# Two layers and four recurrence heads written out on every engine, in place of engine loops

## The chip, the core and the metric

The kernel runs on one core of one Trainium2 chip. The metric is the device time of one execution in microseconds (us). The core has five engines with a sequencer each: PE (TensorE), DVE (VectorE), ACT (ScalarE), POOL (GpSimd) and SP (SyncE, which only issues transfers here). The engines have no common program order; they meet only by semaphores.

## The reference

A decoder trunk of two layers over 16 meta tokens and 1024 real ones (L = 1040 positions, width 1024, float32). Cut to what matters:

```python
for layer in range(DEPTH):                                   # DEPTH = 2
    u = _rmsnorm(h, norm_mix[layer])
    proj = u @ w_in[layer]                                   # columns split among three mixers
    hq, hf, hi, hg, dq, dk, dv, fq, fk, fv, ff = jnp.split(proj, split_at, axis=-1)
    o_a = _hgrn2(hq, hf, hi, hg, ...)                        # gated linear recurrence, 4 heads of 128
    o_b = _diff_attn(dq, dk, dv, ...)                        # two softmax maps, 4 heads of 64
    o_c = _fox_attn(fq, fk, fv, ff, ...)                     # forgetting attention, 4 heads of 64
    h = h + jnp.concatenate([o_a, o_b, o_c], axis=-1) @ w_out[layer]
    u = _rmsnorm(h, norm_ffn[layer])
    h = h + _hier_moe(u, ...)                                # top group of 4, then top 2 of its 8 experts
h = _rmsnorm(h, norm_final)
```

The recurrence is S_t = diag(f_t) S_{t-1} + (1 - f_t) i_t^T, o_t = S_t^T q_t, computed chunk by chunk. The experts are SwiGLU blocks of 1024 to 512 to 1024.

## The kernel before

Each engine has one function that holds its whole program, in an order written out by hand; no scheduler moves anything. Sequence positions are cut into T = 9 tiles (16 rows, then eight of 128). A layer is seven phases, and at the end of each every engine but SP's side cases passes `meet`: it adds to the semaphore `met` when its queue is drained and waits until all have done so.

The phases in the order of the program are: the recurrence, head after head (`project` at L1116 for two projections, L1318 for the other two, then nine blocks: PE computes `levels`, a transpose, the outputs and the state's increment at L1335 to L1365; DVE masks and sums them in `within` at L2015 to L2022 and updates the state at L2039; ACT copies out of PSUM at L943 and L947); the value projection; attention of eight heads (PE: `scores` L1212, `turn_weights` L1237, `outputs` L1250, and pieces of the next heads' projections in between at L1141 to L1175; DVE: row maxima L1827, `join` L1837 to L1843, `turned` L1853; ACT: exponentials L809, `turned` L820, `copy_out` L834); the output projection L1439; routing; the experts, two to a round, 17 rounds in each layer, whose number is only known on the chip; and the sum of both experts' rows with the next norm.

Before the change the layers are one hardware loop on each engine (`with pe.Fori(0, depth) as layer`), the recurrence's heads a loop inside it (`with pe.Fori(0, HEADS) as head`), the rounds of experts a third one with a count from memory. The eight attention heads and all tiles are Python loops, so their code is written out. Semaphores only ever count up, so a wait's value depends on the layer and the head, as in

```python
t = layer * HEADS + head
pe.wait_ge(h_at, ONE + t * T + j + 1)
```

```python
def wait_alone(engine, semaphore, value):
    engine.wait_ge(semaphore, value)
    engine.sem_inc(passed, 1)
```

which is an EVENT_SEMAPHORE of its own (L575) behind the FUSED_REGOPS (L574). `Steps.settle` (L222) is DVE's and ACT's wait for their own earlier instruction.

Of the kernel before, what the change touches and what calls it, by code (L numbers as in the profile page):

```python
# [41 lines left out]
HEADS = 4  # L42
# [185 lines left out]
def build(nc, A, out, stop=PHASES, depth=DEPTH):  # L228

    nc.disable_value_cache = True  # L230
    with ExitStack() as ctx:
# [5 lines left out]
        def signal(name):  # L237

            return ctx.enter_context(nc.semaphore(name))
# [268 lines left out]
        met, passed = signal("met"), signal("passed")  # L508
# [62 lines left out]
        def wait_alone(engine, semaphore, value):  # L571

            engine.wait_ge(semaphore, value)  # L574
            engine.sem_inc(passed, 1)  # L575

        def all_met(layer, phase):

            return layer * ((PHASES - 1) * ENG - 1) + (phase + 1) * ENG - 1

        def meet(engine, layer, phase):

            engine.sem_inc(passed, 1)
            engine.drain().then_inc(met, 1)  # L585
            wait_alone(engine, met, all_met(layer, phase))
# [4 lines left out]
        def _(sp):  # L591
# [19 lines left out]
            ):  # L611
                sp.dma_start(dst, src).then_inc(s_par, 16)

            with sp.Fori(0, depth) as layer:

                if stop > 1:

# [7 lines left out]
                if stop > 1:  # L625
                    def load_qk(n):
                        b = n % 2 if n < HEADS + 2 else 1
                        at = BAND_DA + n * 2 * AW
                        w = A["w_in"][layer].rearrange("(k p) c -> p k c", k=KD)
                        sp.dma_start(w_qk[b], w[:, :, at:at + 2 * AW]).then_inc(t_w[b], 16)  # L630

                    load_qk(0)
                    load_qk(1)
                    with sp.Fori(1, HEADS) as head:
                        t = layer * HEADS + head
                        w = A["w_in"][layer].rearrange("(k p) c -> p k c", k=KD)

                        wait_alone(sp, h_q, ONE + t)
                        sp.dma_start(w_fq, w[:, :, bass.ds(head * 4 * HW, 2 * HW)]).then_inc(h_wfq, 16)
                        wait_alone(sp, h_ig, ONE + t * T)  # L640
                        sp.dma_start(w_ig, w[:, :, bass.ds(head * 4 * HW + 2 * HW, 2 * HW)]).then_inc(h_wig, 16)

                    wait_alone(sp, h_q, ONE + layer * HEADS + HEADS)
                    wait_alone(sp, h_ig, ONE + layer * HEADS * T + HEADS * T)
                    if stop > 2:
                        w = A["w_in"][layer].rearrange("(k p) c -> p k c", k=KD)
                        sp.dma_start(w_v, w[:, :, BAND_V:BAND_FF]).then_inc(v_w, 16)
                    meet(sp, layer, 1)
# [74 lines left out]
        def _(act):  # L723
# [151 lines left out]
                act.wait_ge(own, ONE + turn + 1)  # L875
                act.activation(rstd[:, :], lnss[:, :], ACT.Exp, scale=-0.5).then_inc(done, 1)

            with act.Fori(0, depth) as layer:

                meet(act, layer, 0)  # L880

                if stop > 1:
                    wait_alone(act, s_clean, layer * CLEANS + 2)
                    with act.Fori(0, HEADS) as head:
                        t = layer * HEADS + head

                        def copy_ig(j):
# [208 lines left out]
        def _(pe):  # L1097
# [190 lines left out]

            for j in range(T):
                norm_turn(0, 0, j)  # L1290
            with pe.Fori(0, depth) as layer:
                meet(pe, layer, 0)

                if stop > 1:
                    with pe.Fori(0, HEADS) as head:
                        t = layer * HEADS + head
                        pe.wait_ge(h_wfq, t * 16 + 16)
                        pe.wait_ge(h_at, ONE + t * T)
# [289 lines left out]
        def _(pool):  # L1589
# [10 lines left out]
            for b in range(SLOTS // P):  # L1600
                pool.dma_start(xg[b * P:(b + 1) * P, :].rearrange("p (a n) -> p a n", n=P),
                               zeros.unsqueeze(1).to_broadcast([P, D // P, P])).then_inc(s_zfill, 16)
            with pool.Fori(0, depth) as layer:

                wait_alone(pool, met, all_met(layer, 0))
                for phase in range(1, min(5, stop)):
                    if phase == 2:

                        wait_alone(pool, f_d, ONE + layer * 8 + 8)
                        pool.dma_start(decay_rows[0], dh.bitcast(F32)).then_inc(f_st, 16)  # L1610
                        pool.dma_start(decay_rows[1], dl.bitcast(F32)).then_inc(f_st, 16)
                        wait_alone(pool, f_st, layer * 32 + 32)
                    meet(pool, layer, phase)
                if stop > 5:
                    wait_alone(pool, s_zfill, 16 * (SLOTS // P))
                    meet(pool, layer, 5)
                if stop > 6:
                    before = pool.value_load(pairs[0:1, 1:2], min_val=0, max_val=ROUNDS)
                    count = pool.value_load(pairs[0:1, 0:1], min_val=1, max_val=ROUNDS)

                    def fetch(k, i, nth):

                        n = P if k == 0 else SMALL
                        pool.tensor_copy(pick[0:n, k:k + 1], ids[k][0:n, bass.ds(i, 1)]).then_inc(m_pick, 1)
                        wait_alone(pool, m_pick, ONE + nth)
                        pool.indirect_dma_start(
                            out=xb[0:n, k, :], out_offset=None, in_=u_rows[:, :],
                            in_offset=bass.IndirectOffsetOnAxis(ap=pick[0:n, k:k + 1], axis=0)).then_inc(m_x[k], 16)

                    turns, picks = before * 3 + 2 * layer, before * 2 + 2 * layer  # L1630
                    wait_alone(pool, r_u, (layer + 1) * 16 * T)
                    fetch(0, 0, picks + 1)
                    wait_alone(pool, m_xt, ONE + turns + 2)
                    fetch(0, 1, picks + 2)
                    with pool.Fori(0, count) as i:
                        t = before + i
                        turns, picks = t * 3 + 2 * layer + 2, t * 2 + 2 * layer + 2
                        wait_alone(pool, m_xt, ONE + turns - 2)
                        fetch(1, i, picks + 1)
                        wait_alone(pool, m_xt, ONE + turns + 3)  # L1640
                        fetch(0, i + 2, picks + 2)
                    wait_alone(pool, m_x[0], (before + count) * 16 + layer * 32 + 32)
                    meet(pool, layer, 6)
                if stop > 7:
                    for j in range(T):

                        if j == T - 1:
                            wait_alone(pool, c_h, ONE + T + layer * T + 1)
                        for k in range(2):
                            pool.indirect_dma_start(  # L1650
                                out=ya[0:rows(j), j % (T - 1), k, :], out_offset=None, in_=xg[:, :],
                                in_offset=bass.IndirectOffsetOnAxis(ap=dest[0:rows(j), k, j:j + 1], axis=0))\
                                .then_inc(c_y[j // 2], 16)
# [3 lines left out]
        def _(v):  # L1657
# [265 lines left out]
                finish(ALL - 1)  # L1923
                v.wait_ge(t_out, ONE + layer * ALL + ALL)

            with v.Fori(0, depth) as layer:

                meet(v, layer, 0)

# [1 line left out]
                if stop > 1:  # L1931
# [2 lines left out]
                    v.memset(AT, 0.0).then_inc(s_clean, 1)  # L1934
                    v.wait_ge(s_clean, layer * CLEANS + 2)
                    wait_alone(v, h_const, layer * 32 + 32)
                    with v.Fori(0, HEADS) as head:
                        t = layer * HEADS + head
                        hg.begin(t)
                        lbc = lb[:, bass.ds(layer, 1), bass.ds(head, 1)].rearrange("p a b -> p (a b)")  # L1940
# [542 lines left out]
```

## Time and profile before

| what | value |
|---|---|
| median of 3 runs | 3539.92 us (3539.03 to 3543.38) |
| profiled execution | span 3537.6 us from first to last instruction; its own time is not given apart, the median lies 2.3 us over the span |
| PE busy | 3146.2 us, 89% of the span |
| DVE, ACT, POOL busy | 43%, 23%, 5% |
| granted TensorE clock, mean | 0.924 |
| chain that ended last | PE 71%, DVE 11%, DMA 7%, issue 6% |
| phases of layer 1 (from the chain and the windows) | recurrence 36.7 to 387, attention 401 to 939, output projection to 1076, routing to 1154, experts to 1725, sum and norm to 1787.75 |

### The profile page before, as it was taken

The numbers are of one execution on the slowest core, as the hardware profiler recorded it, in microseconds if no ns is written. First come the engines' busy times: TensorE is split into PE (matmuls) and PEld (weight loads), VectorE is DVE, ScalarE is ACT, GpSimd is POOL, SyncE is SP. The second block draws the span as 40 slices with busy tenths as digits, with TensorE's granted clock in tenths as the row PEclk, the third lists the DMA queues.
The fourth block names the chain that finished last, engine by engine and source line by source line (L and its number), as shares of the span: only waits on it lengthen the run. The fifth ranks groups of instructions, "written<-read, shape, count | busy, mean of one in ns | idle before, by whom it ended". The sixth has DMA issues, their size and how long they took to land.

```text
span 3537.6 us, 50939 instructions
## 1 busy us (share of the span) xinstructions
PE 3146.2 (89%) x16912; PEld 2020.5 (57%) x16912; DVE 1528.3 (43%) x2623; ACT 829.5 (23%) x1917; POOL 168.5 (5%) x239
## 2 busy tenths in 40 slices
PE   7999888898895999999689997888998949999995
PEld 5666456676543555555356664566765435555553
DVE  4666435644325232323446663355543252333324
ACT  4333124432110111111233331344321101111113
POOL 1300000000000000000200000000000000000002
PEclk9999999888896999999889999997978969999997
DMA  5910100001003999999710000000010049999996
GB/s 162 254 51 12 43 13 7 8 7 60 12 30 135 405 406 409 409 410 405 301 37 24 24 24 26 7 7 8 15 52 12 36 182 409 406 408 413 408 411 253
DMA packets 136560, 592.59 MB, mean 168 GB/s; under 512 B 13000, under 2 KB 47816, under 8 KB 119016
## 3 DMA queue, kind: packets, MB, share of 16 engines
q1 hardware_dynamic: 105688, 491.42, 35.4%
q0 software_dynamic: 20400, 72.69, 6.2%
q10 hardware_dynamic: 10336, 26.75, 2.0%
q8 instruction: 76, 1.25, 0.1%
q14 instruction: 60, 0.49, 0.0%
HBM read 524.56 MB, written 66.26 MB: 167 GB/s over the span
## 4 chain that ended last, share of the span: by engine, by line
PE 71%; DVE 11%; DMA 7%; issue 6%; ACT 3%; DVEq 1%; POOL 1%; POOLq 0%; ACTq 0%; SPq 0%
PE ps L1116 7%; PE ps L1439 6%; PE ps L1517 6%; PE ps L1523 6%; PE ps L1157 6%; PE ps L1558 5%; PE ps L1548 5%; DMA arena<-w 4%; PE ps L1250 4%; PE ps L1395 3%; PE ps L1212 3%; PE ps L1237 3%; PE ps L1575 2%; PE ps L1335 2%; DMA arena<-u_rows,arena 2%
## 5 line engine op out<-in xcount | busy, mean ns | idle before, releaser
L1157 PE MATMUL ps<-arena 128*128 128x260 f32 x1024 | 289.9, 416 | 4.6 <-DVE arena L1760 2.8
L1116 PE MATMUL ps<-arena 128*128 128x512 f32 (+1 forms) x768 | 259.4, 496 | 7.3 <-ACTq L585 3.6
L1827 DVE TENSOR_REDUCE negmax<-ps 16x1 f32<-16x16 f32 (+8 forms) x216 | 151.3, 704 | 253.9 <-PE ps L1217 253.2
L809 ACT ACTIVATE arena<-ps,negmax 16x16 f32<-16x16 f32 (+8 forms) x216 | 150.8, 699 | 433.6 <-DVE negmax L1827 432.9
L1517 PE MATMUL ps<-arena 128*128 128x512 f32 x544 | 246.5, 606 | 4.4 <-DMA arena<-w 2.1
L1318 PE MATMUL ps<-arena 128*128 128x256 f32 x1024 | 229.6, 382 | 14.4 <-ACT arena L902 14.4
L1558 PE MATMUL ps<-arena 128*64 128x256 f32 x2176 | 242.3, 381 | 0.0
L1523 PE MATMUL ps<-arena 128*128 128x256 f32 x1088 | 240.4, 379 | 0.0
L1548 PE MATMUL ps<-arena 128*128 128x512 f32 x544 | 239.1, 592 | 0.0
L1523 PEld LDWEIGHTS ps<-arena 128*128 128x128 f32 x1088 | 206.7, 190 | 42.6 <-issue 16.3
L1439 PE MATMUL ps<-arena 128*128 128x512 f32 x512 | 222.4, 592 | 0.0
L1318 PEld LDWEIGHTS ps<-arena 128*128 128x128 f32 x1024 | 191.9, 190 | 49.6 <-ACT arena L902 24.0
L1157 PEld LDWEIGHTS ps<-arena 128*128 128x128 f32 x1024 | 189.6, 201 | 42.0 <-issue 20.5
L1558 PEld LDWEIGHTS ps<-arena 128*64 128x64 f32 x2176 | 153.3, 137 | 99.4 <-issue 25.8
L1250 PE MATMUL ps<-arena 128*64 128x128 f32 (+2 forms) x1440 | 203.2, 321 | 7.1 <-ACT arena L834 3.2
L1116 PEld LDWEIGHTS ps<-arena 128*128 128x128 f32 x768 | 130.5, 196 | 137.4 <-issue 134.1
L1517 PEld LDWEIGHTS ps<-arena 128*128 128x128 f32 x544 | 102.0, 193 | 148.2 <-issue 148.2
L1212 PE MATMUL ps<-rounded 128*128 128x512 f32 (+4 forms) x600 | 178.1, 400 | 3.6 <-ACT arena L809 3.6
L1237 PE MATMUL ps<-ident,arena 128*128 128x128 f32 (+2 forms) x720 | 141.5, 314 | 43.9 <-DVE arena L1853 37.5
L2324 DVE TENSOR_SCALAR arena<-arena 128x512 f32<-128x512 f32 x34 | 14.5, 427 | 374.3 <-ACT arena L1042 374.3
L1548 PEld LDWEIGHTS ps<-arena 128*128 128x128 f32 x544 | 100.7, 190 | 113.8 <-issue 113.8
L1439 PEld LDWEIGHTS ps<-arena 128*128 128x128 f32 x512 | 96.0, 190 | 114.8 <-issue 114.8
(345 smaller groups left out, 4182.7 us busy)
## 6 DMA issues: line engine op xcount, KB each, us to landing
arena<-w SPq DMA_DIRECT2D x204, 2048.0 KB, 20.7
xg<-arena POOLq DMA_DIRECT2D x51, 512.0 KB, 12.2
xg<-arena ACTq DMA_DIRECT2D x34, 512.0 KB
arena<-w_in SPq DMA_DIRECT2D x16, 1024.0 KB, 5.6
xg<-arena ACTq DMA_DIRECT2D x68, 128.0 KB, 9.5
arena<-w_in SPq DMA_DIRECT2D x16, 512.0 KB, 4.0
arena<-w_out SPq DMA_DIRECT2D x2, 4096.0 KB, 13.2
u_rows<-arena SPq DMA_DIRECT2D x16, 512.0 KB, 2.6
```

Source lines behind the costliest of these rows:

```text
L1116: mm = pe.matmul(dst[0:hi - lo, a:b], w[:, k, lo:hi], uT[:, k, a:b], start=(k == 0), stop=(k == KD - 1))
L1157: mm = pe.matmul(out, w_qk[b][:, k, :], uT[:, k, lo:hi], start=(k == 0), stop=(k == KD - 1), skip_group_check=True)
L1212: mm = pe.matmul(flat[0:r, side + x:side + y], q[:, cols(j)], k[:, x:y], start=(i == 0), stop=False, skip_group_check=True)
L1237: mm = pe.transpose(ps[0:rows(i), 5, m * P:m * P + r], weights_in(n, j, 0)[0:r, cols(i)], ident[0:r, 0:r])
L1250: mm = pe.matmul(ps[half:half + AW, 7, at:at + r], V[0:rows(i), i, n * AW:(n + 1) * AW], WT[0:rows(i), g % 3, m * P:m * P + r], start=(i < ...
L1318: mm = pe.matmul(ps[0:r, 6 + j % 2, 0:2 * HW], uT[:, k, cols(j)], w_ig[:, k, :], start=(k == 0), stop=(k == KD - 1), skip_group_check=True)
L1439: mm = pe.matmul(ps[:, 3 * (j % 2) + half, :], mT[:, j % 2, k, :], w_o[:, k, half * 512:half * 512 + 512], start=(k == 0), stop=(k == KD - ...
L1517: mm = pe.matmul(ps[:, 0, :], XT[:, c, :], W1[0][:, c, :], start=(c == 0), stop=(c == KD - 1))
L1523: mm = pe.matmul(ps[:, 1 + q, 0:F // 2], XT[:, c, :], W3[0][:, c, q * F // 2:(q + 1) * F // 2], start=(c == 0), stop=(c == KD - 1))
L1548: mm = pe.matmul(ps[:, 3 + half, :], GT[:, c, :], W2[0][:, c, half * 512:half * 512 + 512], start=(c == 0), stop=(c == KF - 1))
L1558: mm = pe.matmul(ps[q * SMALL:(q + 1) * SMALL, 0 if w is W1 else 1, 0:F // 2], XS[:, c, :], w[1][:, c, q * F // 2:(q + 1) * F // 2], start ...
L1827: v.tensor_reduce(negmax[0:r, at:at + 1], flat[0:r, side:side + wide_], AX.X, ALU.max, negate=True)\
```

## The change

`layer` and `head` become Python numbers on all five engines: the loop over the layers is written out twice, and the recurrence's loop over its heads four times in each. Every wait outside the rounds of experts then has a constant value. The loop over the rounds stays, with its registers. `wait_alone` drops its increment where the value is constant.

```diff
@@ -572,7 +572,8 @@
             engine.wait_ge(semaphore, value)
-            engine.sem_inc(passed, 1)
+            if not isinstance(value, int):
+                engine.sem_inc(passed, 1)
@@ -611,7 +612,7 @@
-            with sp.Fori(0, depth) as layer:
+            for layer in range(depth):
@@ -631,7 +632,7 @@
-                    with sp.Fori(1, HEADS) as head:
+                    for head in range(1, HEADS):
...
@@ -1288,12 +1289,12 @@
-            with pe.Fori(0, depth) as layer:
+            for layer in range(depth):
                 meet(pe, layer, 0)
                 if stop > 1:
-                    with pe.Fori(0, HEADS) as head:
+                    for head in range(HEADS):
                         t = layer * HEADS + head
```

The same two edits stand on ACT and DVE, and the first of them on POOL. No matmul, vector operation or transfer is added, removed or moved against another.

PE, one block of the recurrence before (h_ktTc: ACT has copied the transposed keys; h_at: DVE has made the block's attention matrix; h_igc, h_oc: ACT's copies of the projections and of the output; h_S: DVE has the state):

```order
L1351 ISA
L1352 MATMUL ps<-ident,arena 128x128 [waits h_ktTc]
L1354 ISA
L1355 ISA [waits h_at]
L1356 ISA [waits h_igc]
L1358 ISA [waits h_oc]
L1359 MATMUL ps<-arena 128x128 [waits h_S]
L1361 MATMUL ps<-arena 128x128
L1364 ISA
L1365 MATMUL ps<-arena 128x128 [waits h_ktTc]
```

The same place of the change (all its lines are one higher):

```order
L1353 MATMUL ps<-ident,arena 128x128 [waits h_ktTc]
L1360 MATMUL ps<-arena 128x128 [waits h_oc,h_S,h_igc,h_at]
L1362 MATMUL ps<-arena 128x128
L1366 MATMUL ps<-arena 128x128 [waits h_ktTc]
```

```order
L574 ISA
L1175 MATMUL ps<-rounded,gamma_r 128x260 [waits t_qa]
L1176 MATMUL ps<-rounded,gamma_r 128x260
L1235 ISA
L1237 MATMUL ps<-ident,arena 128x128 [waits t_WT]
L1237 MATMUL ps<-ident,arena 128x128 x3
L574 ISA
L574 ISA [waits t_WT]
L1250 MATMUL ps<-arena 64x128 [waits t_oc]
L1250 MATMUL ps<-arena 64x128 x3
L574 ISA
L1168 ISA [waits t_qa]
```

The same place of the change:

```order
L1176 MATMUL ps<-rounded,gamma_r 128x260 [waits t_qa]
L1177 MATMUL ps<-rounded,gamma_r 128x260
L1238 MATMUL ps<-ident,arena 128x128 [waits t_WT]
L1238 MATMUL ps<-ident,arena 128x128 x3
L1251 MATMUL ps<-arena 64x128 [waits t_oc,t_WT]
L1251 MATMUL ps<-arena 64x128 x3
L1170 MATMUL ps<-arena 128x260 [waits t_raw,t_qa]
```

All register instructions are gone, and with them the EVENT_SEMAPHORE behind each L574, which these rows don't show.

DVE in the attention of the last heads before (t_T: PE has turned the weights; t_pv: PE has read the buffer; t_S: scores are ready):

```order
L1850 ISA
L1851 ISA [waits t_T]
L1853 COPY arena<-ps 128x512 [waits t_pv]
L1850 ISA
L1851 ISA [waits t_T]
L1853 COPY arena<-ps 128x128 [waits t_pv]
L1826 ISA
L1827 TENSOR_REDUCE negmax<-ps 128x1 [waits t_S]
```

The same place of the change:

```order
L1854 COPY arena<-ps 128x512 [waits t_pv,t_T]
L1854 COPY arena<-ps 128x128 [waits t_pv,t_T]
L1828 TENSOR_REDUCE negmax<-ps 128x1 [waits t_S]
```

The two register instructions of each copy are gone, and one EVENT_SEMAPHORE that holds the second wait takes their place. In the built programs PE has 960 register instructions and 427 EVENT_SEMAPHORE before, 48 and 756 after, but before they stand inside loops; its whole program goes from 4078 instructions to 7898, ACT's from 1351 to 1971, DVE's from 1859 to 2654.

## Rows read from the trace of the kernel before

**Rows 1.** The page: busy time and shares; granted clock and DMA in 40 slices.
```profile
PE 3146.2 (89%) x16912; PEld 2020.5 (57%) x16912; DVE 1528.3 (43%) x2623; ACT 829.5 (23%) x1917; POOL 168.5 (5%) x239
PEclk9999999888896999999889999997978969999997
DMA  5910100001003999999710000000010049999996
```

**Rows 2.** Windows of attention (both layers, one weak stretch), experts: us, busy us, PEclk, DMA share.
```profile
401.00:943.00 542.00, 472.00 (x2498) 337.97 (x2497) 250.41 (x540) 172.94 (x481) 1.06 (x2) 0.89 0.05 16
880.00:920.00 40.00, 34.93 (x187) 24.43 (x184) 16.98 (x36) 8.86 (x27) 0.00 (x0) 0.71 0.00 1
1154.00:1725.00 571.00, 564.31 (x2752) 326.46 (x2752) 169.15 (x199) 64.68 (x133) 36.27 (x65) 1.00 1.00 401
2153.00:2700.00 547.00, 478.22 (x2494) 342.61 (x2493) 249.92 (x538) 172.87 (x481) 1.10 (x2) 0.87 0.05 16
```

**Rows 3.** Source lines L574, L575, L1355: duration ns min/median/max, first and last start.
```profile
L574 PEldq FUSED_REGOPS  x1010: 37/37/152, 35.3 to 3483.7; - x169
L575 PEldq EVENT_SEMAPHORE  x1010: 51/51/51, 35.9 to 3488.7; - x169
L1355 PEldq FUSED_REGOPS  x72: 102/103/103, 102.3 to 2127.2; - x72
```

**Rows 4.** Waits in the attention of layer 1: us in total, times, longest.
```profile
PEld ps L1250 <- issue: 32.8, 136, 0.9
```

**Rows 5.** Chain in time, attention: start us, us, what.
```profile
490.81 0.05 ACTq L772
...
924.64 0.03 issue
924.67 0.05 DVEq L1851
924.71 0.04 issue
924.76 0.70 DVE arena L1853
925.46 0.04 issue
925.50 0.66 PE ps L1237 x4
...
941.07 0.05 DVEq L2103
```

**Rows 6.** Chain in time, recurrence, head 1's projections to its level operands.
```profile
155.43 0.10 ACTq L927
155.53 0.05 issue
...
160.10 0.03 issue
160.13 0.13 DVEq L1983
160.26 0.05 issue
```

**Rows 7.** Timeline of one block of the recurrence, [idle before <-releaser].
```profile
192.88 0.63 DVE L2015 TENSOR_TENSOR ps<-ps,arena 128x448 f32<-128x448 f32 x1
193.10 0.30 PEld L1359 LDWEIGHTS ps<-arena 128*128 128x128 f32 x2 [0.19 <-DVE arena L2039]
193.42 0.21 DVE L2018 COPY arena<-ps 64x64 f32<-64x64 f32 x1
193.66 1.26 DVE L2022 TENSOR_REDUCE arena<-ps 64x64 f32<-64x448 f32 x2
194.95 0.35 DVE L2039 SCALAR_TENSOR_TENSOR arena<-arena,glast,ps 128x128 f32<-128x128 f32 x1
195.22 0.63 DVE L2015 TENSOR_TENSOR ps<-ps,arena 128x448 f32<-128x448 f32 x1
```

**Rows 8.** Chain in time around the layer's start, first and second layer.
```profile
35.39 0.53 DVEq L585
35.92 0.80 issue
36.72 1.22 PE ps L1116
...
1784.29 0.07 ACTq L878
1784.36 2.42 issue
1786.78 0.03 ACTq L878
```

**Rows 9.** Source lines L1291 and L1296: branches of the layers' and the heads' loop.
```profile
L1291 PEldq COMPARE_BRANCH  x2: 77/1705/3333, 1782.3 to 3534.5; - x2
L1296 PEldq COMPARE_BRANCH  x8: 76/214/242, 121.7 to 2127.8; - x8
```

More of the change, by code:

```diff
@@ L876, in head_rstd @@
                 act.activation(rstd[:, :], lnss[:, :], ACT.Exp, scale=-0.5).then_inc(done, 1)
-            with act.Fori(0, depth) as layer:
+            for layer in range(depth):
                 meet(act, layer, 0)
@@ L884, in _ @@
                     wait_alone(act, s_clean, layer * CLEANS + 2)
-                    with act.Fori(0, HEADS) as head:
+                    for head in range(HEADS):
                         t = layer * HEADS + head
@@ L1290, in _ @@
                 norm_turn(0, 0, j)
-            with pe.Fori(0, depth) as layer:
+            for layer in range(depth):
                 meet(pe, layer, 0)
                 if stop > 1:
-                    with pe.Fori(0, HEADS) as head:
+                    for head in range(HEADS):
                         t = layer * HEADS + head
@@ L1602, in _ @@
                                zeros.unsqueeze(1).to_broadcast([P, D // P, P])).then_inc(s_zfill, 16)
-            with pool.Fori(0, depth) as layer:
+            for layer in range(depth):
                 wait_alone(pool, met, all_met(layer, 0))
@@ L1924, in attend_dve @@
                 v.wait_ge(t_out, ONE + layer * ALL + ALL)
-            with v.Fori(0, depth) as layer:
+            for layer in range(depth):
                 meet(v, layer, 0)
@@ L1936, in _ @@
                     wait_alone(v, h_const, layer * 32 + 32)
-                    with v.Fori(0, HEADS) as head:
+                    for head in range(HEADS):
                         t = layer * HEADS + head
```

## The prediction

> **What bounds the kernel now.** I read the page first, for which engine could be the bound at all: PE is busy for 89% of the span, DVE for 43%, ACT for 23% [rows 1]. The digits of the clock fall below 9 in the middle of each layer, and those of the DMA stand at 9 only in one quarter of each layer. So the kernel is at least two kernels, and I cut it with windows [rows 2]. In the experts the DMA engines are busy for a share of 1.00 over 571 us and PE for 564: weights set that stretch, PE is as good as full too, and its clock is whole. In the attention the DMA has a share of 0.05, DVE works for 250 of 542 us, ACT for 173, PE for 472 at a clock of 0.89; the second layer's is alike (478 of 547). There PE stands still for 70 and 69 us while it waits to and fro with DVE and ACT. Attention is what register work could be delaying. The third view is the chain in order of time, to see what such a wait is made of; the fourth the single source lines of the sequencer's instructions, since the page doesn't count them.
>
> **What a register wait costs.** One FUSED_REGOPS lasts 37 ns on PE in its short form and 103 in its long one (a layer and a head in the value), an EVENT_SEMAPHORE 51 [rows 3]. That they run costs nothing by itself: a sequencer works ahead of its engine. They cost where one of them has to wait for a semaphore, because then everything behind it is held, and after the release the register work still has to be done before the engine starts. In the chain such a handoff shows as four pieces: PE's transposes end at 924.64, DVE's copy starts 120 ns later, behind 0.03 issue, 0.05 DVEq L1851 and 0.04 issue; back to PE, where the wait is on the matmul itself, it takes 40 ns [rows 5]. So about 0.08 us of 0.12 is the register instruction.
>
> **The change part by part.**
>
> *Attention, PE.* Each `outputs` is preceded by one or two pairs L574 and L575, of which the profile has 1010 [rows 3]. PE's weight loads of L1250 stood idle 136 times in this stretch for "issue", that is for nothing but the sequencer, 32.8 us in all or 0.24 each [rows 4]. One pair is 37 + 51 = 88 ns, with some 30 ns to pass from one to the next (the pieces between in [rows 5]) 0.12. After the change the usual case is one constant wait on the matmul itself and no pair; where t_oc stands beside t_WT one EVENT_SEMAPHORE stays, which is about what a second pair costs now. I take one pair saved at each of the 136: 136 x 0.12 = 16 us. Bounds: nothing, if each gap is the array's own pace between matmuls, and 32.8 if all of it is sequencer.
>
> *Attention, DVE and ACT.* I count 46 pieces like those of [rows 5] on layer 1's chain in the attention, 27 on DVE and 19 on ACT, the first at 490.81 us and the last at 941.07 [rows 5]. An EVENT_SEMAPHORE takes the FUSED_REGOPS's place where two waits meet, so 0.07 us each at best: 3 us. Bounds 0 and 46 x 0.12 = 5.5. Attention thus gives 19 us a layer, 38 in both.
>
> *Recurrence, blocks.* Here PE's order loses the most: six long register instructions in a block, of which L1355, L1356 and L1358 stand in a row, 3 x 103 ns and the passes between. PE indeed idles for 0.19 us before L1359 [rows 7]. But the same rows show DVE without an idle bracket: 0.63, 0.21, 1.26 and 0.35 us, one behind the other, and the next block's L2015 starts 2.34 us after the last. Its register instructions lie under its own running operations. DVE sets the block, and a faster PE waits for it: I cost the 56 inner blocks at 0. If DVE only looks full, the three instructions that become two would save some 0.3 a block, 17 us.
>
> *Recurrence, edges of a head.* On the chain are 0.15 us at L927 and 0.18 at L1983 [rows 6], less the 40 ns that any handoff takes; about twice that again lies at the first block (before DVE is saturated) and at the last. I take 0.75 a head, 6 us for eight; bounds 2 and 10.
>
> *Start of a layer.* PE's first matmul starts 0.80 us after the drain in layer 1, behind a branch and five register instructions. In layer 2 the chain has 2.42 us of issue between ACT's branch and its next MOVE [rows 8], and PE's branch lasts 3.33 us instead of 0.08 [rows 9]. Written out, no engine branches back here. I take 0.7 and 2.6, together 3.3. The page "Runtime: NRT & Kernel Launch" of the Trainium skill, section "Instruction fetch mechanics", says that a taken branch out of a window of two 16 KiB pages forces a fetch before execution goes on. By that rule the heads' loop on PE, 24 KB long, might pay as well; the trace has at most 0.24 us for it [rows 9], and PE has work queued in that time, so the rule's larger sum (six times about 3 us more) is not taken.
>
> *Meets, SP, POOL, output projection, routing.* Their waits are short or under other work: 3 us for 14 meets and the tails of both recurrences (bounds 1 and 6). Nothing in the rounds of experts changes but a term of the layer, and the weights set them: 0.
>
> Sum: 38 + 0 + 6 + 3.3 + 3 = 50 us. The profiled span of 3537.6 us becomes 3487.6; with the 2.3 us that the median lies above it, 3490.
>
> **The rivals.**
>
> *More than that (3450).* Each microsecond that PE no longer idles in attention could also keep its clock up. A mean of 0.89 and 0.87 says that it is at the lower level, 1.2 instead of 2.4 GHz, for 22% and 26% of the two stretches, 119 and 142 us [rows 2]. If a quarter of these goes back to the full level, 65 us of work take half as long, 32 less; with half of the recurrence's bound of 17 for its blocks that is 40, so 3450. For: the weak stretches are those in which PE idles. Against: DVE's full row.
>
> *Mostly hidden (3525).* The gaps before L1250 are then the array's pace, and what PE gains is given to waits for ACT's and DVE's operations, which don't get shorter. Remain the layer's start 3, edges 6, handoffs 3 and meets 3: 15 us. For: PE's FUSED_REGOPS mostly run while matmuls are queued. Against: the 136 gaps have no releaser.
>
> *Instruction fetch takes it back (3540, no change).* The changed program is longer: three more copies of each head's body, twice, are some 15 pages of 256 instructions over PE, DVE and ACT, that before were run from what was loaded. If each cost the 3.33 us of the branch [rows 9] that would be 50 us, all of the gain. Against: attention is straight code already, of which thousands of instructions are run without a gap of that size, and in layer 2 everything is loaded again today.
>
> *Slower (3585).* Attention holds a mean clock of 0.89 and 0.87, but in 880 to 920 us only 0.71, with PE hardly less busy than elsewhere [rows 2]. If a changed rhythm of short bursts and waits took the mean to 0.80, 475 us of PE's work would become 0.88/0.80 of that, 47 us a layer more, 95 in both against 50 gained. It decides from a mean of 0.835 downwards. Nothing in the change makes gaps longer, so it is unlikely.
>
> **How the numbers follow.** Forecast 0.66, more 0.14, mostly hidden 0.13, fetch 0.04, slower 0.03. The forecast's own range is 3465 to 3515, from attention's two bounds taken by halves. To leave out no more than 2 in 10 the whole range reaches toward both neighbours: 3456 to 3522. Less than 0.2% (7 us) can't be told from no change in this kernel. Faster 0.92 (the first three, less 0.01 for a hidden case hidden further), same 0.05, slower 0.03.
>
> **What would show it.** Right: attention some 20 us shorter in each layer at PE busy about the same; the wait of L1250 for issue falling from 32.8 to about 17; L1851's piece gone or replaced by one of 0.02; blocks of the recurrence still 2.34 us apart, with more idle before L1359; layer 2's first L1116 within about 1 us of ACT's last copy; rounds of experts as long as before. Wrong: blocks clearly shorter than 2.34 (DVE was held by its registers after all), an attention that moves by under 8 us or over 35, gaps of 1 us and more on PE with no releaser in heads 1 to 3 (fetch), or a mean clock in attention away from 0.88 by more than 0.03.

## The result and the profile after

The changed kernel takes 3513.07 us in the median of four runs (3501.87 to 3519.85), the kernel before 3541.65 beside it (3539.03 to 3561.24). The ratio of the runs that were timed beside each other is 0.9901 with a 95% interval of 0.9876 to 0.9927: 35 us less (26 to 44); the two medians differ by 28.6. One execution of the kernel before, in the last set of runs below, was disturbed (4214.6 us at a clock of 0.72) and stands in no other figure. The profiled execution took 3514.0 us with a span of 3511.6, 26.0 less than the span of before. I had forecast 3490, 50 us less.

The page of the changed kernel, to be held against [rows 1] (all lines of the code are one higher now): its head, the chain by engine, the clock in 40 slices, and the queue that loads instructions.

```profile
span 3511.6 us, 44842 instructions
...
PE 3132.8 (89%) x16912; PEld 2012.4 (57%) x16912; DVE 1527.0 (43%) x2623; ACT 830.8 (24%) x1917; POOL 169.7 (5%) x239
...
PEclk8999999897796999999889999997987969999997
...
q8 instruction: 94, 1.54, 0.2%
...
PE 67%; DVE 17%; DMA 8%; ACT 4%; issue 4%; POOL 1%; POOLq 0%; SPq 0%; ACTq 0%; DVEq 0%; PEldq 0%
```

The same engine instructions are executed, and every engine's busy time is the same but PE's, which is 13 us less. Issue on the chain has gone from 6% to 4%, and DVEq from 1% to 0%. In layer 1's attention the chain of before has 184 pieces with DVEq or ACTq, 8.7 us of them, and that of the changed kernel 24, 0.5 us. DVE's share rose from 11% to 17%, in part because the chain of the recurrence's blocks, which ran through PE's matmuls before (134.8 of 139 us), runs through DVE's operations now (99.0). The windows say where the time went (window, its length in us, busy us of PE, PEld, DVE, ACT, POOL, the mean granted clock, DMA share): attention of both layers, the weak stretch, the experts.

```profile
399.94:937.53 537.59, 474.26 (x2575) 339.69 (x2572) 251.93 (x543) 173.77 (x481) 1.06 (x2) 0.89 0.05 16
2140.76:2681.66 540.90, 479.01 (x2575) 342.76 (x2572) 252.08 (x543) 173.78 (x481) 1.11 (x2) 0.88 0.05 16
...
1143.00:1720.00 577.00, 565.88 (x2759) 326.64 (x2758) 168.80 (x198) 64.36 (x132) 37.49 (x66) 1.00 0.99 396
879.00:919.00 40.00, 34.89 (x196) 24.63 (x192) 17.49 (x36) 7.97 (x23) 0.00 (x0) 0.72 0.00 1
```

[Rows 2] have windows that end elsewhere. With the same two landmarks, from the first L1157 to the first L1439, the kernel before shows:

```profile
400.76:948.65 547.89, 477.89 (x2575) 340.99 (x2571) 252.11 (x543) 173.21 (x481) 1.06 (x2) 0.88 0.05 16
2152.04:2706.12 554.08, 485.30 (x2574) 346.47 (x2571) 252.17 (x543) 173.23 (x481) 1.10 (x2) 0.87 0.05 16
```

So attention is 10.3 and 13.2 us shorter, 23.5 of the 26. Of these PE's idle time (length less busy, both layers) makes 13.6, from 138.8 to 125.2, and its busy time 9.9. The rest by landmarks: the recurrence, from L1116's first to L1374's first matmul, is 352.9 and 353.4 us before, 353.1 and 352.4 after; the first layer's start is 0.9 us shorter, the second's with the norm before it 2.4 (59.8 to 57.4); the experts, from the first L1517 to the last L1575, 592.0 and 589.9 before, 595.8 and 589.3 after, a change that I don't count, since the kernels below have 588 to 599 there, with nothing altered in the experts.

Two readings of single waits. First the row that my largest term rested on, [rows 4], in the changed kernel (engine, line, what it waited for, us, times, longest):

```profile
PEld ps L1251 <- issue: 28.5, 123, 0.5
```

It had 32.8 us and 136 times. I had it fall to 17. In the trace of before matmuls are running during 29.9 of the 32.8 us, so that PE itself stands still for 2.8 of them; in the changed kernel it does for 0.9. Second, the handoff of [rows 5], PE's transposes to DVE's copy and back, in the chain (start us, us, what):

```profile
904.97 0.23 PE ps L1238
905.20 0.02 issue
905.22 0.70 DVE arena L1854
905.92 0.04 issue
905.97 0.90 PE ps L1238 x3
```

DVEq L1851 and one issue of it are gone: 20 ns where 120 were.

Start of the second layer, as [rows 8], and one block of the recurrence on DVE, as [rows 7] (start us, us, engine, line):

```profile
1776.72 0.02 ACT arena L1091
1776.74 0.06 issue
1776.81 0.56 ACTq L586
1777.36 0.04 issue
1777.40 2.07 PE ps L1117 x2
```

```profile
191.58 0.63 DVE L2016 TENSOR_TENSOR ps<-ps,arena 128x448 f32<-128x448 f32 x1
191.77 0.30 PEld L1360 LDWEIGHTS ps<-arena 128*128 128x128 f32 x2 [0.24 <-issue]
...
192.11 0.21 DVE L2019 COPY arena<-ps 64x64 f32<-64x64 f32 x1
192.35 1.26 DVE L2023 TENSOR_REDUCE arena<-ps 64x64 f32<-64x448 f32 x2
...
193.64 0.35 DVE L2040 SCALAR_TENSOR_TENSOR arena<-arena,glast,ps 128x128 f32<-128x128 f32 x1
...
193.90 0.63 DVE L2016 TENSOR_TENSOR ps<-ps,arena 128x448 f32<-128x448 f32 x1
```

ACT's last copy is followed by a matmul after 0.66 us where 2.42 of issue lay alone; this block takes 2.32 us instead of 2.34 (in the median of all 2.33 instead of 2.34), with PE's weight loads idle for 0.24 before its output instead of 0.19.

### The profile page after: what moved, and what is told of

Read it like the earlier page. It is cut to its first block, busy times and chain, and to the rows that moved or that the text cites. A ratio compares the mean times of both kernels' runs of the same rounds, so it can differ in the third digit from the quotient of the medians.

```text
span 3511.6 us, 44842 instructions
## 1 busy us (share of the span) xinstructions
PE 3132.8 (89%) x16912; PEld 2012.4 (57%) x16912; DVE 1527.0 (43%) x2623; ACT 830.8 (24%) x1917; POOL 169.7 (5%) x239
## 3 DMA queue, kind: packets, MB, share of 16 engines
q8 instruction: 94, 1.54, 0.2%
## 4 chain that ended last, share of the span: by engine, by line
PE 67%; DVE 17%; DMA 8%; ACT 4%; issue 4%; POOL 1%; POOLq 0%; SPq 0%; ACTq 0%; DVEq 0%; PEldq 0%
PE ps L1117 7%; PE ps L1518 7%; PE ps L1524 6%; DMA arena<-w 6%; PE ps L1440 6%; PE ps L1158 6%; PE ps L1559 5%; PE ps L1549 4%; PE ps L1251 4%; PE ps L1396 3%; PE ps L1213 3%; PE ps L1238 3%; PE ps L1576 2%; DVE negmax L1828 2%; PE ps L1319 2%
```

## The experiments

Twelve kernels were timed in interleaved rounds beside the kernel before. Its median was 3545.66 us beside *layers_only*, *pe_only*, *dve_act_only* and *keep_increment* (23 runs), 3547.43 beside the four with more register instructions in the attention (31), and 3542.17 beside *late_last*, *heads_only* and the two of the recurrence (35). Ratios are given with their 95% intervals.

### Which part: layers, heads, engines, increments

*layers_only*: the loop over the layers is written out on all engines, the four heads of the recurrence stay a loop.

```diff
-            with pe.Fori(0, depth) as layer:
+            for layer in range(depth):
...
                     with pe.Fori(0, HEADS) as head:
```

> The layers are written out on every engine, the recurrence's four heads stay a loop; waits of attention, projection and routing are constants, those of the recurrence still come from a register. If the gain sits in the attention and at the layer's start, as the two traces suggest (attention 10 and 13 us shorter, start 3.4), this kernel keeps nearly all of it: span 3512 to 3516, attention 528 and 531 us, layer 1's recurrence as before at 353 us from the first L1116 to the first L1374. Rival (my forecast's 0.75 us at each head's edge, or a code path that is only good in one straight piece): span 3518 to 3525, with the loss in the recurrence. Rival (the loop over heads costs instruction fetch): the recurrence 1 to 3 us longer a head than with everything written out.

It took 3515.97 us, a ratio of 0.9917 (0.9897 to 0.9937); the span of the profiled run is 3509.8. The heads are 85.43, 85.36 and 85.38 us long, no longer than with everything written out. The whole gain is there within the intervals; writing out the heads has no part that can be seen. The clock has none either: the mean granted clock over the runs is 0.9212, against 0.9210 of the kernel before beside it.

*heads_only*: the complement, the recurrence's heads written out, the layers a loop.

```diff
             with pe.Fori(0, depth) as layer:
...
-                    with pe.Fori(0, HEADS) as head:
+                    for head in range(HEADS):
```

> The recurrence's four heads are written out on every engine, the layers stay a loop, so that all values still come from a register of the layer, and every branch of the heads' loop is gone. With the layers alone written out the whole gain was there already (ratio 0.9917), so this should give nothing that can be measured: within 4 us of before, heads of 85.3 to 85.9 us. My forecast's term for the edges of a head (0.75 us each) would be 2 to 6 us, if the branch rather than the register values were its cause. If it is slower by more than 5 us, the longer program costs something by itself.

It took 3552.92 us, 1.0020 (1.0002 to 1.0038). There is no gain, as expected, but a trace of a loss, to which I come with the clock. The recurrence is 354.9 and 355.1 us long.

*pe_only* has both edits on PE alone.

> Only PE is written out, in layers and heads; DVE, ACT, POOL and SP keep their loops and register values. Theory A (PE's register instructions and the pairs L574 and L575 hold PE's sequencer in the attention): most of the gain stands, attention 530 and 534 us, span 3516 to 3522. Theory B (the handoffs count, that is the register instruction behind each release on DVE and ACT): PE gives little, attention 535 and 541, span 3528 to 3534. In both the recurrence stays at 353 us a layer, since DVE sets its blocks.

It took 3532.61 us, 0.9959 (0.9941 to 0.9977), 14 us less (8 to 21). That is neither theory's number, but about half of the gain.

*dve_act_only* has them on DVE and ACT alone.

> Only DVE and ACT are written out, in layers and heads; PE, POOL and SP keep their loops. The mirror of the kernel with PE alone. Theory A (PE's sequencer): little here, attention 536 and 542 us, span 3530 to 3535. Theory B (handoffs on DVE and ACT): most of the gain, attention 531 and 535 us, span 3518 to 3524. If the two halves add up to the whole (26 us of span), the costs lie one behind the other on one chain; if each alone gives nearly all, one hides the other; if each gives little, both must go together.

It took 3533.78 us, 0.9961 (0.9945 to 0.9977), 14 us less (8 to 20), again about half. The two halves add up to about 28 of the 29 to 35 that the kernels with all engines win. So PE's share and that of DVE and ACT lie one behind the other as far as these intervals tell, and are of one size. My forecast for the attention had 32 to 6. The mean clock is 0.9208 and 0.9207 in these two, as good as that of before.

*keep_increment*: everything written out, but the helper keeps its increment for constants too.

```diff
             engine.wait_ge(semaphore, value)
-            if not isinstance(value, int):
-                engine.sem_inc(passed, 1)
+            engine.sem_inc(passed, 1)
```

> Everything is written out as in the changed kernel, but a wait through the helper still adds one to its own semaphore, so on PE some 1010 EVENT_SEMAPHORE of 51 ns stay, now in front of every output, and none of these waits can ride on a matmul. If the instruction behind the pair is what held PE (half of the pair's time), half of the attention's gain is lost: attention 533 and 537 us, span 3520 to 3526. If the register instruction alone held it, attention 529 and 532 us, span within 3 us of 3511.6. If PE's sequencer runs so far ahead that neither counts, the same 3511.6.

It took 3513.87 us, 0.9906 (0.9884 to 0.9928), which can't be told from the changed kernel. Yet the row before the outputs is almost that of before:

```profile
PEld ps L1250 <- issue: 31.7, 129, 0.8
```

So 3 us more of "issue" in that row cost nothing that the times can tell. Matmuls are running during 28.8 of these 31.7 us: nine tenths of the row are idle time of PEld, not of PE. That the EVENT_SEMAPHORE behind the wait is free is not shown. PE idles for 129.3 us in both attentions against 125.2 in the changed kernel, and the mean clock of this kernel's six runs is high, 0.9242 against 0.9210 beside it, so a price of some 5 us may be hidden.

### Number of register instructions, or their place

Four kernels are the one before with more register instructions. "Again" says the last wait of a handoff twice, so that one more register instruction is held by the semaphore and executed behind its release; "ahead" puts about as many of the same kind in front (on PE 456 a layer to 434), behind a wait that has long been met.

```diff
                     v.wait_ge(t_T, ONE + G0 + g + 1)
                     v.wait_ge(t_pv, ONE + G0 + g - 2)
+                    v.wait_ge(t_pv, ONE + G0 + g - 2)      # again_dve_act
...
+                    v.wait_ge(met, ONE + layer * 3)        # ahead_dve_act
                     v.wait_ge(t_T, ONE + G0 + g + 1)
                     v.wait_ge(t_pv, ONE + G0 + g - 2)
```

> The kernel before, with the last wait of each handoff of the attention said twice on DVE (maxima, join, turned) and on ACT (exponentials, turned, copies out): 240 more register instructions a layer on each, each of them released together with the operation and executed before it. In the trace of before, DVE and ACT stood idle until the release at 517 such places over both layers (143 at the maxima, 191 at the exponentials, 98 and 69 at the two turned, 16 at the copies out), and there an operation with one register wait starts 38 ns after the release, with two waits 116 to 133. Theory 1 (what counts is register work behind the release): each place is 80 to 95 ns later, 44 us in all; since DVE and ACT written out alone took 25 us of such delays away and won some 14 of time, about 0.55 of it reaches the end: 24 us longer, about 3570. Theory 2 (it is the number of sequencer instructions, wherever they stand): this kernel and the one with the same instructions ahead of the wait are longer by the same amount. Theory 3 (the delays on DVE and ACT are hidden by matmuls): within 5 us of before.

It took 3562.39 us, 1.0047 (1.0028 to 1.0066), 17 us more (10 to 23). This is the handoff in its chain:

```profile
933.04 0.97 PE ps L1240 x4
934.01 0.03 issue
934.03 0.05 DVEq L1856
934.08 0.05 issue
934.13 0.05 DVEq L1857
934.18 0.04 issue
934.22 0.70 DVE arena L1859
```

Two register instructions and their passes stand between the transposes and the copy, 0.21 us.

> The kernel before, with the same number of register instructions added at the same places on DVE and ACT (240 a layer on each), but ahead of the handoff's own waits, behind a wait that has long been met, so that they are done before the release comes. Theory 1 (register work behind the release): within 5 us of before, and handoffs of 38 and 116 to 133 ns as before. Theory 2 (their number): as long as the kernel that says the last wait twice, 20 us and more. One reservation: where the handoff has a single wait, its value is now computed by an instruction that carries a wait that is met, so nothing of it lies behind the release.

It took 3545.20 us, 0.9993 (0.9974 to 1.0012). There is no change, with the same number of instructions. Theory 2 is out.

> The kernel before, with PE's last wait said twice ahead of scores, turned weights, outputs and the pieces with t_raw and t_parts: 434 more register instructions a layer on PE, behind the release. PE stands idle for a release at some 50 places a layer (14 before L1237 for DVE, 16 before L1175 for ACT, and singles). If only those count, 0.09 us at each of them in both layers: 5 to 10 us longer, about 3553. If PE's sequencer is the pace of the outputs, as my forecast had it (16 us a layer for one pair at each of 136 gaps before L1250), every instruction of 37 ns and its pass counts where PE's weight loads wait for issue: at 0.12 each on 136 gaps, 33 us longer, about 3578.

It took 3567.55 us, 1.0058 (1.0036 to 1.0080), 21 us more (13 to 28). That is between the two numbers that I gave, 5 to 10 and 33.

> The kernel before, with 456 register instructions a layer added on PE at the same places, but ahead of the waits, behind one that has long been met. If PE's sequencer runs ahead of the array and only work behind a release counts: within 5 us of before. If its pace counts: as long as the kernel that says PE's last wait twice, or longer.

It took 3549.40 us, 1.0010 (0.9990 to 1.0029): 456 register instructions a layer more change nothing that can be told. So PE's sequencer isn't the pace either: what counts on PE is also mainly what stands behind a release. That again_pe cost more than my 5 to 10 us is not for idle places that I had missed: PE's idle time in both attentions grew by 9.8 us, which is what 50 places a layer at 0.09 us give. In its profiled run the rest of attention's 21.1 us is 4.2 us of work at the full clock level and 7.1 that its lower level adds (the table of three parts below).

How late an operation starts behind its release can be worked out for every place of the attention at which DVE or ACT stood idle for it, from the end of the releasing operation and the start of the released one in the trace. Medians in ns, places over both layers:

| place | before | after | again_dve_act | ahead_dve_act | late_last |
|---|---|---|---|---|---|
| DVE maxima behind PE, one wait | 38 (143) | 38 (141) | 133 (143) | 37 (143) | 37 (144) |
| DVE turned behind PE, two waits | 133 (98) | 38 (96) | 229 (96) | 133 (96) | 37 (100) |
| ACT turned behind PE, two waits | 118 (69) | 37 (72) | 195 (61) | 118 (70) | 37 (73) |
| ACT exponentials behind DVE, one or two | 116 (191) | 35 (194) | 192 (190) | 116 (193) | 35 (193) |

This is the mechanism, as the table and the two pairs of kernels show it: a single register wait costs nothing that can be told, since its value is computed ahead and the operation itself carries the wait. Of two waits in a row the first is carried by the register instruction of the second, and when that first one is the late one, 95 ns on DVE and 80 on ACT lie behind the release. By the Trainium skill's page "Perfetto Trace Analysis", sections "Sequencer-only Instruction (DRAIN, etc)" and "DVE / Act Engine Instruction (TENSOR_ADD, Activation, etc)", a sequencer waits itself for a control instruction's semaphore, while an engine's operation waits in a queue of its own and the sequencer goes on; the table agrees. Summed over these places the change takes 25 us of such delays away on DVE and ACT (38.2 in the last three rows before, 13.1 after).

### The same handoffs without any writing out

*late_last*: if the place is all, the order of the waits should do. This is the kernel before, with all its loops; where two or more waits stand in a row on DVE and ACT in the attention, the one met long before comes first.

```diff
-                    v.wait_ge(t_T, ONE + G0 + g + 1)
                     v.wait_ge(t_pv, ONE + G0 + g - 2)
+                    v.wait_ge(t_T, ONE + G0 + g + 1)
```

> The kernel before with all its loops and register values, and only the order of two or more waits in a row changed on DVE and ACT in the attention: the wait that is met long before comes first, the late one last, so that it is the operation itself that carries the late one and the register instructions are done ahead of it. No instruction is added or taken away. Theory 1 (what counts is register work behind the release): turned on DVE starts 38 ns behind PE instead of 133, turned on ACT 38 instead of 118, the exponentials 35 instead of 116, and the kernel wins what DVE and ACT written out alone won, some 14 us: 3525 to 3540 against about 3546. Theory 2 (it is the number of register instructions or the loops' branches): no change, and the gain of DVE and ACT written out alone came from elsewhere.

It took 3552.73 us, 1.0029 (1.0013 to 1.0046), 10 us *more* (5 to 16). The handoffs became exactly what I expected (the last column of the table), and the time went the other way. The windows say what happened in the profiled run; attention in late_last:

```profile
403.78:957.68 553.90, 487.32 (x2575) 348.56 (x2571) 252.02 (x543) 173.57 (x481) 1.05 (x2) 0.86 0.05 16
2161.32:2718.71 557.39, 492.46 (x2575) 351.72 (x2571) 252.45 (x543) 173.84 (x481) 1.10 (x2) 0.86 0.05 16
```

PE's idle time is 131.5 us over both layers, 7.3 less than before, as in dve_act_only (131.3). But PE is busy for 16.6 us more, at a granted clock of 0.86 instead of 0.88 and 0.87. The lower clock is not one run's luck: over its 12 runs the mean clock is 0.9165, over the 35 of before in the same rounds 0.9219, which is 40 us more of the execution at the lower level (2 x 0.0835 x 3552 against 2 x 0.0781 x 3542). heads_only shows the same, 0.9174 and 34 us.

Whether the clock explains the whole is open. In the three sets of runs of the kernel before, a thousandth of the mean clock goes with 1.6 to 2.1 us of time, so the 0.0054 are worth 9 to 11 us. That is the 10 us lost, but not the gain of 7 to 14 as well that the shorter handoffs should have brought. For heads_only the same estimate gives 7 to 9 us, and 7 were measured.

### Attention in three parts

The trace's clock records are either at the full level (2.4 GHz) or at half (1.2 GHz). With PE's busy time at half level I can split the length of each attention: PE idle, its work as if all at full level (busy less half of the busy time at half level), and what the half level adds. Sums over both layers, us, each from the windows of the profiled run:

| kernel | length | PE idle | work at full level | added by half level |
|---|---|---|---|---|
| before | 1102.0 | 138.8 | 843.4 | 119.8 |
| after | 1078.5 | 125.2 | 840.7 | 112.6 |
| layers_only | 1084.8 | 123.9 | 839.8 | 121.1 |
| keep_increment | 1082.1 | 129.3 | 839.6 | 113.2 |
| pe_only | 1095.6 | 129.1 | 839.7 | 126.8 |
| dve_act_only | 1104.8 | 131.3 | 841.0 | 132.5 |
| late_last | 1111.3 | 131.5 | 840.3 | 139.5 |
| heads_only | 1125.3 | 137.9 | 840.8 | 146.5 |
| ahead_dve_act | 1105.3 | 137.0 | 842.8 | 125.4 |
| ahead_pe | 1110.7 | 140.4 | 844.0 | 126.2 |
| again_pe | 1123.1 | 148.6 | 847.6 | 126.9 |
| again_dve_act | 1123.1 | 153.0 | 846.1 | 124.0 |

PE's idle time orders the kernels by what was done to them, to within some 2 us if the two kernels with instructions ahead (137.0 and 140.4 against 138.8) are the measure. The work at full level moves by 8 us at most. What half level adds moves by 34 us without order, and is what makes a single profiled attention a poor witness: dve_act_only's is longer than that of before in this one execution, though the kernel is faster over twelve.

### How well the recurrence's register work is covered

*again_rec_pe* and *again_rec_dve* say four waits of a block twice, on PE or on DVE.

```diff
                             if j > 0:
                                 pe.wait_ge(h_S, ONE + t * (T - 1) + j)
+                                pe.wait_ge(h_S, ONE + t * (T - 1) + j)
```

> The kernel before, with four of PE's waits in a block of the recurrence said twice (h_at ahead of the levels, h_ktTc ahead of the transpose and of the state's increment, h_S ahead of the output), some 270 more register instructions of 103 ns over both layers. If DVE sets the block and PE's register work lies under it, as I forecast, blocks stay at 2.34 us, the recurrence at 353 us a layer and the kernel within 5 us of before. If PE's register work is on the path, 4 x 0.13 us a block over 64 blocks are 33 us more.

It took 3546.76 us, 1.0012 (0.9995 to 1.0029): within what I expected for the kernel, but not for the block. These are DVE's mask operations of two blocks, one after the other:

```profile
197.17 0.63 DVE L2019 TENSOR_TENSOR ps<-ps,arena 128x448 f32<-128x448 f32 x1
...
199.65 0.63 DVE L2019 TENSOR_TENSOR ps<-ps,arena 128x448 f32<-128x448 f32 x1
```

They start 2.48 us apart instead of 2.34: of the 0.52 us (4 x 0.13, an estimate) that was added to PE's order in a block, 0.14 comes through, and the starts of the 36 mask operations of a layer lie 3.9 us further apart in sum. So PE has about 0.4 us of slack in a block and not more.

That the kernel's time hardly shows these 8 us of two layers is at least in part the clock's doing. From the first mask operation of one head to that of the next, the windows show (length, busy us of PE, PEld, DVE, ACT, POOL, granted clock) two heads of before, then one of again_rec_pe:

```profile
187.18:272.65 85.47, 81.82 (x598) 57.50 (x600) 53.74 (x85) 28.92 (x52) 0.00 (x0) 0.98 0.08 25
272.65:356.67 84.02, 80.38 (x598) 56.89 (x600) 53.74 (x85) 28.91 (x52) 0.00 (x0) 1.00 0.04 12
188.76:273.91 85.15, 80.92 (x600) 56.96 (x602) 54.33 (x86) 28.91 (x52) 0.00 (x0) 1.00 0.08 25
```

In before four of six such heads have the clock at 0.98 and last 85.5 to 85.6 us, and two have it whole and last 84.0. In again_rec_pe five of six have it whole and last 85.15, which is 1.1 more than 84.0. The longer blocks thus reach the head's end in full, and the clock gives back 1.5 us a head. Over its 12 runs the mean clock is 0.9243, against 0.9219 of before.

> The kernel before, with four of DVE's waits in a block of the recurrence said twice (h_lvl, h_o, h_ds, h_S). DVE is the engine that sets the block. If its register instructions are executed under its own running operations (0.63, 0.21, 1.26 and 0.35 us in a row), blocks stay at 2.34 us and the kernel within 5 us of before. If a register instruction that stands between two operations of the bound engine is paid for, 4 x 0.13 us a block over 64 blocks, up to 33 us more; if only the wait for its own last operation (h_S) is exposed, a quarter of that, 8 us.

It took 3545.91 us, 1.0008 (0.9989 to 1.0026). The same sum grows by 1.8 us a layer, and the median block stays at 2.34. DVE's own register instructions lie nearly all under its running operations.

## Why the prediction was right, and where its sizes were off

*Direction, place and mechanism: right.* Attention carries 23.5 of 26 us, by PE idling less between handoffs; experts and the blocks of the recurrence give nothing. That the time fell inside the range, 2 us from its upper end, owes something to luck all the same: the largest term was twice too large, and the second was less than half of what it should have been.

*Attention, PE, "I take one pair saved at each of the 136: 136 x 0.12 = 16 us": the term that was mis-sized.* With both layers it is 32; PE alone gives 14 (8 to 21) in the whole kernel. The gaps before L1250 are PEld's, and nine tenths of them lie beside running matmuls: 32.8 us fell only to 28.5, and stay at 31.7 in keep_increment without a cost that its times show. My lower bound described that row better ("nothing, if each gap is the array's own pace"): PE's own standstill in it fell by 1.9 us in layer 1. What PE does gain comes behind its own releases: its idle time falls by 9.7 us over both layers in pe_only.

*Attention, DVE and ACT, "0.07 us each at best: 3 us": mis-sized the other way.* DVE and ACT alone give 14 us (8 to 20) in the whole kernel, not 6 with the edges apart. The piece cost 95 and 80 ns, and I had counted 46 pieces on layer 1's chain, where the chain has 184 with DVEq or ACTq; the trace has some 290 delayed places over both layers (98, 69, and about 126 of those at the exponentials). Which share of the 25 us reaches the end isn't settled: taking them away by constants won 14, adding about 42 us of them (again_dve_act) cost 17, and taking them away by order won 7.3 us of PE's idle time in the profiled run but nothing of the kernel's time.

*Recurrence, blocks, 0: right.* The median block went from 2.34 to 2.33 us. That the cover would hold against twice the work as well was too much: again_rec_pe.

*Recurrence, edges of a head, 6 us: too much.* The heads are 85.9 to 85.5 us before, 85.6 to 85.2 after, some 0.3 each, and over both layers the recurrence is 0.8 us shorter. The 0.18 us at L1983 is gone, but the runs show no more of the kind. Part of the small term is hidden by the clock: two of six heads of before have it whole (84.0 us between mask operations), and none of the changed kernel's has (85.3 to 85.4).

*Start of a layer, 3.3: right.* It gave 0.9 and 2.4.

*Meets and others, 3:* what lies between attention and experts (187.2 and 186.9 us to 186.7 and 186.6) and behind the last L1575 (54.6 to 54.1) gives 1.3.

*The rival of the clock, "more".* Part of it came: 7.2 of attention's 23.5 us are half-level time given back in the profiled run. But layers_only has none of it in its profile and wins nearly as much over its runs, so I don't count it as an effect of the change. What I put down in its favour, that the weak stretches are those in which PE idles, is not in my own rows: PE is busy for 87% of the stretch at 0.71 and for 87% of the whole attention.

*Mostly hidden:* its argument about the gaps before L1250 was true for nine tenths of their length; it failed because the handoffs were worth more than it allowed.

*Instruction fetch:* the instruction queue moved 1.54 MB in 94 packets instead of 1.25 in 76, 18 more where I had some 15, and no stage is longer but layer 1's experts, by 3.8 us. The Trainium skill's page "Runtime: NRT & Kernel Launch", section "Instruction fetch mechanics", might have had the heads' branches cost as well, if their targets lay outside its window of two pages; heads_only takes them away and the recurrence is not shorter (354.9 and 355.1 us against 352.9 and 353.4), so nothing of that sum is there.

*Slower by clock:* the mean in attention stayed at 0.89 and 0.88. It did fall in late_last, to 0.86, and in heads_only, to 0.85 and 0.86. That is above the 0.835 from which I had it decide against 50 us, but against a gain of 7 or none it can decide the sign.

*The sum, 50:* PE alone and DVE and ACT alone make 28, of which the second layer's start is 1.1 and 1.0. That lies within the 35 (26 to 44) that was measured. The forecast's own range began at 3465 and ended at 3515; the result lies near its upper end, since attention gave 12 us a layer and not 19.

## What to carry to other kernels

A register-valued wait costs time only where its register instruction stands behind a late semaphore: look for pieces with a q in the chain between an operation and the next engine's, and don't count those that run ahead. Of several waits in a row put the late one last (its handoff takes 38 ns instead of 133 here), or make the values constants. Only the constants shortened this kernel: with the order alone it became 10 us longer, at a lower clock. Write out the loop whose variable the hot waits need (here the layers' alone gives it all), not every loop; and read a weight-load "issue" row only together with PE's own idle time.

## What was not expected of the hardware

Small changes in the waits move the granted clock of a whole kernel: 0.9165 in the mean of 12 runs for late_last, 0.9174 for heads_only, 0.9234 and 0.9243 for again_rec_dve and again_rec_pe, against 0.9219 beside them. A thousandth of it is 7 us of the execution at 1.2 instead of 2.4 GHz. In attention PE is busy for nine tenths of such time (111 of 126 us and 129 of 143 before), which by estimate makes 3 us of time; among the runs of the kernel before a thousandth goes with 1.6 to 2.1 us. In every profile the two attentions take about half of it (256 us of 547 after, 270 of 534 before, 324 of 597 in heads_only), while a layer's experts have 3 to 6 us. What in the rhythm decides it stays open: PE idles less in late_last than before, and its clock is lower. So a gain of some 7 us can be covered in this kernel by a shift of the clock that neither the code nor a trace of before foretells.
